# Hybrid attention/convolution block: on VectorE the copy of a transposed probability block is issued ahead of the score step of the same round

## The reference

```python
proj = h @ w_in                         # q, k, v, x_c, gate_b, gate_c
q = rms_norm(q.reshape(B, S, 8, 64)); k = rms_norm(k.reshape(B, S, 8, 64))
# each chunk of 64 queries attends to its own chunk and the 8 before it
s = einsum('bqhd,bkhd->bhqk', qc, kb) * 64 ** -0.5 + bias
p = softmax(where(key_pos >= 0, s, -1e30))
y_attn = einsum('bhqk,bkhd->bqhd', p, vb)
y_conv = gate_b * causal_depthwise_conv(gate_c * xc, w_conv, b_conv)
y = concat([rms_norm(y_attn), rms_norm(y_conv)]);  return y @ w_out
```

## Time and profile before

| what | value |
|---|---|
| runs | 2070.51, 2073.55, 2079.07 us; median 2073.55 |
| profiled execution | 2076.78 us, its span 2075.1 us |
| TensorE busy / mean granted clock | 2000.9 us (96%) / 0.983 |
| VectorE busy | 900.0 us (43%) |
| ScalarE busy | 625.6 us (30%) |
| GpSimd busy | 417.9 us (20%) |
| attention of mixer 1 | from 928 to 1017 us: TensorE busy 75.97 of 89 us, clock 0.87 |
| attention of mixer 2 | from 1195 to 1301 us: TensorE busy 92.99 of 106 us, clock 0.92 |
| a dense matmul of 512 columns | mean 391 ns (it overlaps the next) |

### The profile page before, as it was taken

One profiled execution on the slowest core, in us unless ns is written; L12 is line 12 of the kernel. 1 busy time (PEld: TensorE's weight loads), 2 busy tenths in 40 slices (PEclk: granted clock), 3 DMA queues, 4 the chain that ended last, 5 costly groups with the idle time before them and its releaser, 6 DMA issues. The chain is left out here.

```text
span 2075.1 us, 26383 instructions
## 1 busy us (share of the span) xinstructions
PE 2000.9 (96%) x9300; PEld 1655.2 (80%) x9300; DVE 900.0 (43%) x1135; ACT 625.6 (30%) x863; POOL 417.9 (20%) x384
## 2 busy tenths in 40 slices
PE   4999999999999999998899988999999999999997
PEld 3888878888887888876788877888888888888886
DVE  8733335433333443247553367633333443333333
ACT  2422223222222232324333133333333232222221
POOL 2445553445554000302113020200000000000000
PEclk9999999999999999998999989999999999999998
DMA  8344444444443332222032220232223322222332
GB/s 353 125 151 133 141 122 130 134 141 143 142 139 121 92 101 94 82 81 87 31 104 80 76 87 1 77 106 95 97 93 92 101 99 92 100 96 96 95 116 83
DMA packets 63902, 224.54 MB, mean 108 GB/s; under 512 B 6880, under 2 KB 7008, under 8 KB 63456
## 3 DMA queue, kind: packets, MB, share of 16 engines
q1 hardware_dynamic: 54048, 192.24, 28.2%
q0 software_dynamic: 7488, 27.27, 3.9%
q10 hardware_dynamic: 2304, 4.20, 0.5%
HBM read 219.48 MB, written 4.19 MB: 108 GB/s over the span
## 5 line engine op out<-in xcount | busy, mean ns | idle before, releaser
L721 DVE TENSOR_TENSOR w_lo<-raw,w_hi 128x1024 fp32r<-128x1024 f32 x328 | 430.5, 1313 | 767.2 <-ACT w_hi L498 767.0
L1142 PE MATMUL pair<-h_hi,w_hi 128*128 128x512 f32 x1728 | 682.7, 395 | 8.6 <-DVE h_lo L826 6.5
L1143 PE MATMUL pair<-h_lo,w_hi 128*128 128x512 f32 x1728 | 675.9, 391 | 0.0
L1144 PE MATMUL pair<-h_hi,w_lo 128*128 128x512 f32 x1728 | 675.8, 391 | 0.0
L498 ACT CAST w_hi<-raw 128x1024 fp32r<-128x1024 f32 x336 | 351.7, 1048 | 651.7 <-PE pair L1144 637.4
L1142 PEld LDWEIGHTS pair<-h_hi,w_hi 128*128 128x128 f32 x1728 | 326.7, 189 | 77.0 <-DVE h_lo L826 6.6
L1144 PEld LDWEIGHTS pair<-h_hi,w_lo 128*128 128x128 f32 x1728 | 326.3, 189 | 69.0
L1143 PEld LDWEIGHTS pair<-h_lo,w_hi 128*128 128x128 f32 x1728 | 326.6, 189 | 65.8
L1142 PE MATMUL pair<-hid_hi,w_hi 128*128 128x512 f32 x704 | 274.9, 390 | 0.0
L1143 PE MATMUL pair<-hid_lo,w_hi 128*128 128x512 f32 x704 | 274.0, 389 | 0.0
L1144 PE MATMUL pair<-hid_hi,w_lo 128*128 128x512 f32 x704 | 273.9, 389 | 0.0
(11 more groups left out here) (116 smaller groups left out, 1458.8 us busy)
## 6 DMA issues: line engine op xcount, KB each, us to landing
raw<-w_f1i SPq DMA_DIRECT2D x88, 512.0 KB, 3.6
raw<-w_f2i SPq DMA_DIRECT2D x88, 512.0 KB, 3.4
ada_w<-w_ada POOLq DMA_DIRECT2D x52, 512.0 KB, 3.8
raw<-w_mix SPq DMA_DIRECT2D x48, 512.0 KB, 3.4
raw<-w_f1o SPq DMA_DIRECT2D x32, 512.0 KB, 3.5
raw<-w_f2o SPq DMA_DIRECT2D x32, 512.0 KB, 3.5
ada<-w_ada SPq DMA_DIRECT2D x5, 2048.0 KB, 16.5
raw<-w_mo SPq DMA_DIRECT2D x16, 512.0 KB, 3.5
```

Of the source, the lines that this page charges most:

```text
L721: nc.vector.tensor_tensor(col(w_lo, slot * CW, CW), col(raw, (n % RAW) * CW, CW), col(w_hi, slot * CW, CW).bitcast(F32), ALU.subtract).the ...
L1142: nc.tensor.matmul(dst, lh, rh, start=first, stop=False)
L1143: nc.tensor.matmul(dst, lh, rl, start=False, stop=False)
L1144: return nc.tensor.matmul(dst, ll, rh, start=False, stop=last)
```

## The change

In the VectorE loop of each mixer, from round 4 on, `probs(s-2)` is issued ahead of `scores(s)` instead of behind it. Rounds 2 and 3 keep the old order. All other engines, all waits, tiles and buffers are as before.

```diff
                     for s in range(UNITS + 3):
+                        if 4 <= s < UNITS + 2:
+                            probs(s - 2)
                         if s < UNITS:
                             scores(s)
                         if s == 1:
                             for ct in range(KA):
                                 conv_gate(ct)
-                        if 2 <= s < UNITS + 2:
+                        if 2 <= s < 4:
                             probs(s - 2)
                         if 0 <= s - CONV_SQUARE - 1 < KA:
                             add_square(NORM_CONV[p], s - CONV_SQUARE - 1)
```

## The result

The change makes the kernel slower by about half a percent: median 2089.39 us of 11 runs against 2077.75 of 11 runs of the kernel before, ratio 1.0055 (95% interval 1.0038 to 1.0072). The forecast was +17.9 us, 2092, with a range of 2077 to 2106; measured were +11.6 us, and 2089.4 lies inside the range. The forecast started from a median of 2073.55 of three runs of the kernel before; over 11 runs it is 4.2 us higher. The profiled execution took 2093.04 us with a span of 2091.4, against 2076.78 and 2075.1.

A forecast was written before the change was run, and what follows sets the result against it. Bound: a closed loop of TensorE and VectorE, 5.68 us per pair of rounds at full clock. Terms (a) to (e), 4.2 + 4.2 + 2.8 - 2.3 + 9 = +17.9 us on 2073.55, gave 2092; range 2077 to 2106.

The forecast's parts named there:

- the likeliest case: Whole kernel: slower by +13 to +27 us, its own range 2087 to 2101 us; chance 0.52.
- the two waits: TensorE: transposes' wait for the copy falls from 21.0 to under 8 us; score matmul's for the score step rises from 2.8 to above 20.
- VectorE's idle time ahead of `y_low`: Round 16: VectorE's idle time ahead of `y_low` stays near 0.7 us.
- The bare exchange: Undisturbed pair of rounds: even rounds gain, odd rounds lose, loop 5.67 against 5.68 us, so it costs what it did.
- (b): Rounds 16 and 24: `y_low` waits for ScalarE's split with the odd copy queued behind; +1.5 each mixer 2, 0.6 mixer 1; +4.2 us.
- (a): Even rounds: VectorE's side work no longer fits and runs over by about 0.3 us, 14 times; +4.2 us.
- (c): TensorE insertions in even rounds: less gap to gain; rounds 8 and 10 +0.74 and +0.4 per mixer; sum +2.8 us.
- (d): TensorE insertions in odd rounds: `y_turn` of rounds 15 and 23 covers most of the new wait, -1.6 us; stage ends -0.7.
- (e): TensorE's clock in the attention stages: new gaps and idleness bring five more half-clock stretches; +9 us, bounds -5 to +22.
- R1: Rival, waits without the clock: terms (a) to (d) alone, +9 us, 2082; chance 0.24.
- R2: Rival, the exchange is even: side work and `y_low` find room after all, within 4 us, 2074; chance 0.12.
- R3: Rival, the copy's release decides: each of 24 transpose waits shrinks by up to 0.75, -18 us, 2056; chance 0.04.

The follow-up runs named there:

- e5: Kernel before with `y_low` moved one round later (rounds 17, 25, 33), old order kept: 2075.20 us, ratio 0.9991 to the kernel before.
- e6: Changed kernel with `conv_first`, `conv_second`, `y_norm2`, `y_low` moved to odd rounds, `y_turn` and ScalarE's split one round later: 2080.86 us, 1.0013 of the kernel before.
- e4: Changed kernel with the value product of rounds 17 and 25 issued three times instead of once: 2082.94 us, ratio 1.0011 to the kernel before.
- e1: Kernel before with the copy ahead of the score step in even rounds only: 2072.99 us, ratio 0.9963 to the kernel before.
- e3: Changed kernel with `y_low` alone moved one round later (rounds 17, 25, 33): 2076.43 us, ratio 0.9992 to the kernel before.
- e8: Kernel before with the copy first in even rounds only and `y_low` alone one round later: 2062.87 us, ratio 0.9941 to the kernel before.
- e9: Changed kernel with ScalarE's first two output-weight splits moved from rounds 3 and 4 to 7 and 8: 2085.63 us, ratio 1.0024 to the kernel before.

## Why the prediction was right, and where its terms were off

The direction, the range and the mechanism held: the wait moved from the transposes to the score matmul, and what stands unevenly in the rounds turned an even exchange into a loss. That 2089.4 comes so near 2092 is partly luck. As a difference, +11.6 against +17.9, the forecast was 6 us too high, and below the +13 of the likeliest case; the starting point, 4.2 us too low, made up for most of it.

Of the signs that it named, the two waits (6.8 and 21.0), the gap of 2.46 us and the longer time at half clock came true. Three did not: the plain pair is 5.44 and not 5.6 to 5.8; the rest of the program differs by 3.3 us and not by 1, in a part that no kernel here changes; and VectorE's idle time ahead of `y_low` is 1.46 and not 0.7. The last was a slip against its own chain: the copy that used to fill half of that wait had moved away. By its own terms:

- *The bare exchange* was put at 5.67 against 5.68 per pair. It is 5.44. The step that failed is "0.89 later": I took the copy to start as long after the transposes as the score step does, and it starts 0.12 sooner. At two hand-overs per pair that is 0.25 us, and for some 20 pairs at full clock 5 us (an estimate from these rows). The forecast's waits of 9 us less 5 are 4, against 5.5 read from the runs; the other terms, where they can be read, came out near their size.
- *(b) `y_low`*, +1.5 each in mixer 2 and 0.6 in mixer 1, was right. Its chain was right to 0.02 us. The plain pair beside it is shorter, so removing it is worth 1.9 (7.33 to 5.44); against the old order, where it cost 0.3, that is 1.6. In mixer 1 it is 1.23 for round 24, where the move in the old order is worth 0.59 (3.29 to 2.70, e5): 0.64 net. For round 16 of mixer 1, at half clock in both profiles, the pair takes 5.68 against 5.23 before, 0.45 more.
- *(a) side work in even rounds*, 0.3 each: pairs of 5.78 and 5.84 against 5.44, so 0.34 and 0.40. Right in the pair. One such step was not foreseen: the `add_square` held up by GpSimd. Between the two profiles its pair in mixer 1 is longer by 2.2 us, but with the hold in both orders only by 0.6.
- *(c), (d) TensorE's insertions* were not tested by themselves. But full-clock pairs in the profiles give (c): against the old order rounds 8 and 10 of mixer 2 take 0.53 (5.68 in e5, 6.21 in e6) and 0.61 (5.84, 6.45) more, where +0.74 and +0.4 were put. The pair with `y_turn` and `y_norm2` takes 5.93 in place of 6.08. e6 shows the sign of (d): `y_turn` moved to an even round makes its pair longer.
- *(e) the clock*, +9: +5.0 by the runs' clocks, with some 2 us of doubt, for 15.3 us more at half clock. In the two profiles the stretches went from six to seven and from 41 to 58 us: they became longer rather than more, where I had counted five more. The mechanism was right, the size too large, though well inside the bounds. In the profile both 2.46 us gaps of mixer 2 were followed by such a stretch, and filling the gaps of both mixers took 6.6 us away over the runs.

R1, waits without the clock, is refuted as a full account by e4; as a size, +9, it came nearer to the +11.6 than the forecast did, because the clock and the waits were both overrated. R2's even exchange holds for plain pairs only. R3 was right in its even half and wrong as a whole: e1 has it, at -0.87 per pair, once the odd rounds are left alone. The rule that I set against the trace (find the gaps of the contended engine and make their releaser sooner) promises R3, not "the first rival" as the prediction has it. It would have given the faster kernel if followed with the other wait in view: the gap names one side of a loop.

## What to carry to other kernels

When two steps of one engine release two different waits of another, give each round the order that its own next consumer needs; an exchange in all rounds moves the wait. Count what else is queued behind a moved step, most of all a step that waits for a third engine: one `y_low`, twice per mixer, made the larger part of the loss. A step moved together with the one that it waits for takes its wait along, as `y_low` did with its split in e6; moved alone, in e3 and e8, it waited for nothing. And read a kernel with this clock at equal time at half clock: 0.32 us of time per us of it went with nearly all of the scatter of 21 us here.

## What the runs showed of the hardware that was not expected

- VectorE starts a PSUM-to-SBUF copy 0.77 to 0.80 us after the start of the transposes that it waits for, but the custom score step with a reduction 0.88 to 0.92 us after; e1 has both in one kernel (0.80 and 0.88). Both wait on TensorE; why they differ was not tried.
- More TensorE work made the changed kernel faster: the value product run three times over in each of two gaps per mixer (20 records more in one gap of mixer 2), 2089.4 to 2082.9 us.
- A two-input VectorE addition in SBUF is held while GpSimd runs a two-input subtraction in SBUF (0.68 to 2.81 us), while copies and score steps that read PSUM in the same rounds kept 0.68 to 0.82 (in the changed kernel a copy of 0.69 at 955.14, beside a subtraction that ran from 953.42 to 955.78). The Trainium skill ("SBUF — State Buffer", section Terms) describes an exclusive port pair of the two engines, held for the whole instruction; the trace agrees, and e9 takes the hold away by moving GpSimd's work.
